# Norm sums taken per chunk, token-column roots, no barriers between dense stages, and modulation units in pairs

## The reference

```python
def rms_norm(x, g):
    y = x * lax.rsqrt(jnp.mean(x * x, axis=-1, keepdims=True) + RMS_EPS)
    return y * g

mod_l = jnp.split(c_act @ ada_w[l] + ada_b[l], N_MOD, axis=-1)   # and mod_c from cc_act
h_l = modulate(xl, norm_mix_g[l], mod_l[0], mod_l[1])            # norm(x) * g * (1 + scale) + shift
xl = xl + mod_l[2] * o_l
xl = xl + mod_l[5] * sq_relu_mlp(modulate(xl, norm_mlp_g[l], mod_l[3], mod_l[4]), w_mlp1[l], w_mlp2[l])
return rmsnorm(xl, final_norm_g)
```

## Time and profile before

| | us |
|---|---|
| median of 3 runs | 3123.83 (3122.11 to 3124.45) |
| the profiled execution | 3122.36 |
| its span in the trace | 3120.6 |
| PE busy | 2918.6 |
| DVE / ACT / POOL busy | 860.3 / 716.4 / 237.7 |

### The profile page before, as it was taken

The page is one execution under the profiler, slowest core; times in us unless marked ns, Lnnn a source line. Parts: engine busy times, 40 slices in busy tenths (PEclk is TensorE's granted clock), DMA queues, the critical chain, the costliest instruction groups (busy, mean ns, idle before and its releaser), DMA issues. The chain is left out here.

```text
span 3120.6 us, 30901 instructions
## 1 busy us (share of the span) xinstructions
PE 2918.6 (94%) x12390; PEld 1851.9 (59%) x12390; DVE 860.3 (28%) x1571; ACT 716.4 (23%) x1683; POOL 237.7 (8%) x260
## 2 busy tenths in 40 slices
PE   7989997999997999999989999997999799998998
PEld 6768884455554666444434444443666577787887
DVE  1421003545545333200121110004555523201101
ACT  1420002356455233100010000002454422201100
POOL 3000000223232000000000000000222200000000
PEclk8989998999998999899999999998999999999999
DMA  9328763433331221122214543333344222254552
GB/s 222 88 75 247 223 206 89 110 88 95 95 97 53 55 55 55 48 74 78 73 52 127 149 129 121 101 98 81 103 108 102 75 68 68 81 152 124 151 151 71
DMA packets 529871, 330.42 MB, mean 106 GB/s; under 512 B 27472, under 2 KB 496832, under 8 KB 529728
## 3 DMA queue, kind: packets, MB, share of 16 engines
q1 hardware_dynamic: 518896, 296.36, 33.5%
q0 software_dynamic: 10528, 31.46, 4.1%
q10 hardware_dynamic: 304, 0.61, 0.1%
HBM read 327.05 MB, written 1.34 MB: 105 GB/s over the span
## 5 line engine op out<-in xcount | busy, mean ns | idle before, releaser
L917 PE MATMUL ps<-xnT,W 128*128 128x512 f32 (+2 forms) x4064 | 1341.8, 490 | 65.6 <-ACTq L392 44.0
L917 PEld LDWEIGHTS ps<-xnT,W 128*128 128x128 f32 (+1 forms) x4064 | 776.9, 193 | 597.2 <-issue 469.7
L917 PE MATMUL ps<-BIG,W 128*128 128x256 f32 (+1 forms) x2528 | 773.5, 468 | 11.1 <-ACTq L392 8.5
L917 PEld LDWEIGHTS ps<-BIG,W 128*128 128x128 f32 x2528 | 481.2, 191 | 301.3 <-issue 247.3
L1733 DVE SCALAR_TENSOR_TENSOR TMP<-ps,prmT,TMP 128x510 f32<-128x510 f32 (+3 forms) x256 | 182.6, 714 | 140.9 <-ACT TMP L714 126.4
L552 ACT ACTIVATE xnT<-hT 128x256 f32<-128x256 f32 (+1 forms) x56 | 23.1, 495 | 630.8 <-DVEq L392 630.8
L1653 DVE SCALAR_TENSOR_TENSOR hT<-ps,modc,hT 128x256 f32<-128x256 f32 x48 | 21.7, 481 | 398.1 <-PE ps L917 398.1
L501 POOL DMA_DIRECT2D cs_rows<-BIG x2 | 1.1, 564 | 1693.9 <-DVE BIG L1775 1693.9
L1327 PE MATMUL ps<-W,xnT 128*128 128x128 f32 x1024 | 122.6, 276 | 0.0
L527 POOL TENSOR_TENSOR BIG<-BIG,TMP 128x512 f32<-128x512 f32 x80 | 108.2, 1367 | 186.7 <-ACT BIG L747 186.7
L546 ACT ACTIVATE TMP<-ps 128x512 f32<-128x512 f32 (+4 forms) x130 | 73.2, 569 | 208.7 <-PE ps L1327 94.3
(11 more groups left out here) (248 smaller groups left out, 2172.4 us busy)
## 6 DMA issues: line engine op xcount, KB each, us to landing
W<-in_w_in SPq DMA_DIRECT2D x192, 512.0 KB, 4.0
W<-in_w_mlp SPq DMA_DIRECT2D x128, 512.0 KB, 4.0
W<-in_ada_w SPq DMA_DIRECT2D x96, 512.0 KB, 4.9
BIG<-cs_rows POOLq DMA_DIRECT2D x96, 256.0 KB, 4.8
W<-in_w_ssd_o SPq DMA_DIRECT2D x32, 512.0 KB, 4.0
W<-in_w_gate SPq DMA_DIRECT2D x22, 512.0 KB, 8.3
W<-in_w_up SPq DMA_DIRECT2D x22, 512.0 KB, 6.5
W<-in_w_down SPq DMA_DIRECT2D x16, 512.0 KB, 4.1
```

The source lines that it names most:

```text
L917: last = mm(dst, w[:, c, 0:m], rhs(k), start=k == 0, stop=k == total - 1)
```

## The change

1. *Norms.* The square of a chunk is taken by ACT as soon as its residual is added (in `rooted`), and DVE adds the squares of chunks 0 to 6 into `ssum` between residuals (`summed`). After the last product, PE multiplies 128 token columns at a time, as the stationary side, by one column of ones (`statistic`): the sum over the width lands with one token per partition, in one column per 128 tokens. Root and reciprocal are taken of these 2 or 4 columns; DVE multiplies them into an identity (`diagonal`), and one product with ones spreads them over all partitions (`gap`). The scaling reads this from PSUM. ACT loads the table of the root ahead by a root of a constant.
2. *normf1 and mixnorm0 become one:* both statistics are taken from `hT` (with and without the gain), the second mean is made from the first in columns; the normed output of the first block is made in `hT` by POOL, in two multiplies of 128x2048.
3. *No barriers* but ahead of wout1, att0 and att1. The first product of a stage waits per chunk (`ready`).
4. *The end:* in f21 each chunk is multiplied by the gain and transposed one product later; the copies out of PSUM scale by the reciprocal, two on ACT and two on DVE, followed by four stores.
5. *Modulation units* go in pairs: seven pairs behind steps of dense stages (`MID`), five inside the norms (`GAP`). Inside a norm the rows of the first unit stand in PE's stream between statistic and spreading product, those of the second behind it; the columns follow after two products (or after the first of ssd). ACT copies the rows in place of DVE.

```diff
-ADA = {"ffn1": (0, 0, 8), "down1": (0, 8, 4), "f10": (1, 0, 8), "f20": (1, 8, 4)}
+BARRIERS = {"wout1": 3, "att0": 6, "att1": 9}
+MID = {("ffn1", 5): (0, 2), ("down1", 1): (0, 4), ("wout20", 0): (0, 8), ("f10", 2): (1, 0), ("f10", 5): (1, 2),
+       ("f20", 1): (1, 4), ("wout21", 0): (1, 8)}
+GAP = {"wout1": (0, 0), "down1": (0, 6), "wout20": (0, 10), "f20": (1, 6), "wout21": (1, 10)}
...
+            pool.wait_ge(r1_kept, 1)
+            pool.wait_ge(n_x, 16)
+            h0 = hT[:, :, 0:S]
+            nc.gpsimd.tensor_tensor(h0, h0, r1b[:, :].unsqueeze(1).to_broadcast([P, KC, S]), ALU.mult)
+            pool.drain()
+            nc.gpsimd.tensor_tensor(h0, h0, prmT[:, 0, 16:24].unsqueeze(2).to_broadcast([P, KC, S]), ALU.mult)\
+                .then_inc(h_ready, 1)
...
+            def rooted(ph, n, l=None, which=0):
+
+                A(small[:, 59:60], eps, ACT.Sqrt)
                 for c in range(KC):
+                    act.wait_ge(g_free, freed(ph, c))
+                    last = A(xnT[:, c, 0:n], hT[:, c, 0:n], ACT.Square)
+                    if ph == "down1":
+                        last = A(xnT[:, c, S:T], hT[:, c, 0:S], ACT.Square, scale=prmT[:, 0, 16 + c:17 + c])
+                    last.then_inc(n_sq, 1)
...
+                act.wait_ge(n_col, NORMS[ph] + 1)
...
+                    A(root[:, 0:m], stat[:, 0:m], ACT.Sqrt, scale=1.0 / D, bias=eps).then_inc(n_rt, 1)
+                if ph in GAP:
+                    row_copies(*GAP[ph], which=(0,))
+                if l is not None:
+                    for c in range(KC):
+                        act.wait_ge(n_x, 8 * NORMS[ph] + c + 1)
...
+                        last.then_inc(n_sh, 1)
+                if ph in GAP:
+                    row_copies(*GAP[ph], which=(1,))
...
+            def statistic(ph, m):
+
+                k = NORMS[ph]
+                stat = PS[6 if ph == "f21" else 3]
+                one = cst[:, C_ONE:C_ONE + 1]
+                pe.wait_ge(n_acc, k + 1)
+                for j in range(m):
+                    mm(stat[:, j:j + 1], ssum[:, j * P:(j + 1) * P], one, start=j == 0, stop=False)
+                pe.wait_ge(n_sq, 8 * k + 8)
+                for j in range(m):
+                    last = mm(stat[:, j:j + 1], xnT[:, KC - 1, j * P:(j + 1) * P], one, start=False, stop=j == m - 1)
+                last.then_inc(n_col, 1)
+
+            def gap(ph, m, n):
+
+                l, u = GAP[ph]
+                statistic(ph, m)
+                ada_rows(l, u)
+                pe.wait_ge(n_dg, NORMS[ph] + 1)
+                mm(PS[3][:, 0:n], ones, diag[:, 0:n // P, :].rearrange("p a b -> p (a b)"), start=True, stop=True)\
+                    .then_inc(n_bc, 1)
+                if ph == "down1":
+                    mm(PS[6][:, 0:S], ones, flat(diag1), start=True, stop=True).then_inc(r1_ps, 1)
+                ada_rows(l, u + 1)
...
-                product([("dt", l)], PS[4][0:64, :], xa, 64)
+                product([("dt", l)], PS[4][0:64, :], xa, 64, ready=shifted("f20" if l else "down1"))
...
+            def summed(ph, c, n):
+
+                if c == 0:
+                    return
+                dve.wait_ge(n_sq, 8 * NORMS[ph] + c + 1)
+                if c > 1:
+                    dve.drain()
+                last = V.tensor_tensor(ssum[:, 0:n], xnT[:, 0, 0:n] if c == 1 else ssum[:, 0:n], xnT[:, c, 0:n], ALU.add)
+                if c == KC - 2:
+                    last.then_inc(n_acc, 1)
```

More of the change, by code:

```diff
@@ L322, in build @@
         g1_t, g1_e = sem("gain1_transposed"), sem("gain1_kept")
-        x_sq, x_ms, x_rt, x_sc, x_t, x_e = (
-            [sem(f"x_{n}{t}") for t in range(2)] for n in ("squares", "mean", "root", "scaled", "transposed", "kept"))
+        x_sq, x_ms, x_rt, x_sc, x_t = (sem(f"x_{n}") for n in ("squares", "mean", "root", "scaled", "transposed"))
+        x_e = [sem(f"x_kept{t}") for t in range(2)]
         p_done, p_kept, p_added = sem("piece_done"), sem("piece_kept"), sem("piece_added")
@@ L328, in build @@
         line_ps, line_sb, line_out, bias_in = sem("line_ps"), sem("line_sb"), sem("line_out"), sem("bias_in")
-        n_sq, n_sum, n_ms, n_rt, n_x = (sem(f"norm_{x}") for x in ("squares", "sum", "mean", "root", "scaled"))
+        n_sq, n_acc, n_col, n_rt, n_ms, n_dg, n_bc, n_x, n_sh = (
+            sem(f"norm_{x}") for x in ("squares", "summed", "columns", "root", "second_mean", "diagonal", "spread",
+                                       "scaled", "shifted"))
+        r1_ps, r1_kept, h_ready = sem("first_root_spread"), sem("first_root_kept"), sem("first_normed")
+        n_hg, out_a, out_v = sem("end_gained"), sem("out_by_scalar"), sem("out_by_vector")
         u_sc, u_mx, u_ex, u_pn, u_tp, u_pt, u_pv, u_out = (
@@ L672, in _ @@
             begin(act, "wout1")
-            end(act)
-            squares("norm2", S)
-            end(act)
-            begin(act, "ffn1")
+            rooted("wout1", T)
             for i in range(FC1 // 2):
@@ L1246, in _ @@
                 front(0, 0)
+                pair(ada_columns, GAP["f20" if l else "down1"])
                 front(0, 1)
@@ L1440, in _, with from_merge @@
-            norm("normend", S)
-            begin(pe, "out")
-            for t in range(2):
-                for half in range(2):
-                    for c in range(4):
-                        last = nc.tensor.transpose(PS[2 * t + half][:, c * P:(c + 1) * P],
-                                                   xnT[:, 4 * half + c, t * P:(t + 1) * P], ident)
-                    last.then_inc(out_t, 1)
-            end(pe)
+                def from_merge(k):
+                    pe.wait_ge(m_free, 8 * l + k + 1)
@@ new lines, in _, with transposed @@
+                gap(f"wout2{l}", nt // P, nt)
+                dense(f"f1{l}", 8, single(f"f1{l}"), lambda t: PS[4 + t][:, 0:nt], xn, ready=shifted(f"wout2{l}"),
+                      gapped=f"wout2{l}")
+                def transposed(c):
+                    pe.wait_ge(n_hg, c + 1)
+                    for t in range(2):
+                        last = nc.tensor.transpose(PS[2 * t + c // 4][:, (c % 4) * P:(c % 4 + 1) * P],
+                                                   xnT[:, c, S + t * P:S + (t + 1) * P], ident)
+                    last.then_inc(out_t, 1)
@@ L1770, in masked @@
                             .then_inc(ssd[l, "mready"], 1)
+                adds(*GAP["f20" if l else "down1"])
                 conv(0, 0)
```

389 lines of the change are left out of this document (210 added, 179 removed).

## The result

The changed kernel takes 3001.94 us (median of four runs, 2997.00 to 3004.68) against 3124.14 us for the kernel before (3122.11 to 3125.69): a ratio of 0.9606, 95% interval 0.9591 to 0.9621, or 122.2 us less. The prediction was 3011.0 us, range 2999 to 3034. The profiled execution has a span of 3001.1 us, 119.5 us less than the span of the one before.

The account below looks back on a forecast made before the run. TensorE, busy 2918.6 of 3120.6 us, was taken as the bound. 153.15 + 11.7 - 34.8 - 6.5 - 1.7 - 5 - 4 = 112.85 us less gives 3011.0 us; 8-in-10 range 2999 to 3034.

Parts of the forecast that it names:

- the forecast's own case: Whole kernel: all terms act as summed, 112.85 us less, 3011.0 us, range 3003 to 3020; chance 0.58.
- rival C: Whole kernel: no port conflict or clock loss, less half clock behind dt chain (some 5 us); 2997 us; chance 0.10.
- The norms' chain: Five gaps between dense stages: first products start 6.4, 8.0, 7.3, 7.3 and 5.8 us in, sum 34.8 us.
- rival B: Gaps of the norms: new chain slower than summed, 3 us a gap, total 3026 us; chance 0.17.
- Rival E: Change fails to do what it says, e.g. first products stay behind eighth chunk: 5.7 us more a gap, 3040; chance 0.05.
- The clock in the gaps: Five new gaps: light work drops TensorE's clock in two, 2 us each, 4 in all; bounds 0 and 10.
- Rival A: Five gaps: each wholly at half clock, with loss behind it, 34 us in place of 4, 3041 us; chance 0.08.
- The end: Tail after the last product: 18.42 us become 6.5; transposes moved into f21 cost TensorE 1.7 us.
- The modulation units and short barriers: TensorE outside the gaps: moved units free 11.7 us; five short stretches, mostly bare barriers, 10.55 us, go to zero.
- rival D: Tile ring: refills one behind another at 4.9 us starve unit pairs, 315 us over twelve, 3326 us; chance 0.01.
- GpSimd's multiplies: Start of ssd0: two 2048-column multiplies delay VectorE's dt chain, which TensorE awaits, by 5 us; bounds 0 and 10.2.
- The test named in the prediction's last part: Profile after: if the gaps are as summed and the total is not, a stretch outside the tabled windows has grown.

Follow-up runs that it names:

- the split rows: Against the changed kernel, two of the first unit's four row tiles in each norm issued ahead of the last chunk's statistic: 3001.89 us, ratio 0.9604.
- the repeated kernel: The changed kernel itself, unedited, run and profiled again on another chip: 3000.77 us median, ratio 0.9608, profiled span 2994.8 us.

## Why the prediction was right, and where it was off

The forecast of 112.85 us less stands against 119.5 in the profiled pair and 122.2 in the medians. The measured 3001.94 us lies in the range of 2999 to 3034, but 1 us outside the 3003 to 3020 of the forecast's own case, and nearer to rival C's 2997 than to 3011.0. Set out by place, its terms compare so (the 0.3 us that miss from 112.85 are rounding):

| place | forecast, us less | measured, us less |
|---|---|---|
| the six stretches (130.33) | 85.0 (34.8 + 4 + 6.5 left) | 80.4 (42.6 + 7.3 left) |
| dense stages | 35.4 | 37.6 |
| stages with SSD and attention | -7.9 | 1.5 |
| sum | 112.5 | 119.5 |

The misses have opposite signs: the stretches gave 4.6 us less than forecast, the long stages 9.4 more. That the total came out within 9 us is in part luck.

*The norms' chain.* Right in its parts. Of the 7.8 us by which the five gaps exceed 34.8, some 6.1 are the clock and 1.7 the chain. Without half clock the first, third and last gap read 6.67, 7.76 and 6.06 us for 6.4, 7.3 and 5.8, so the forecast is 0.3 to 0.5 us too low each; rival B had 3. The miss in the third is ahead of the unit rows: the last chunk's statistic starts 1.8 us behind the last product, not 1.5. That chunks arrive fast enough for the products is right: none waits behind a gap, and undoing the per-chunk start costs 26 us. Undoing the early squares costs 43. The second gap (8.0 forecast) had half clock in both profiles, 9.40 and 9.35; at full clock it reads 8.22 in the kernel with the barriers restored. Rival E is excluded by the gaps themselves, and its price was nearly right: 28.5 us, five times 5.7, against 26 in the kernel that does what it describes, where the waits were 5.3 to 5.7 us in three norms and about 2 in the two others.

*The clock in the gaps.* The mechanism was right, the size a little low. Forecast were two of five gaps at 2 us, 4 in all. The first profile has three gaps at about 1.64 and one at 1.2, some 6.1 us; the second has two, 2.8. Rival A (all five cold throughout) did not come: only the first unit's rows and what is beside them fall to the lower level, and the split rows remove even that. The loss behind the gaps, 12.27 us, went in full, as summed. So the sign that the prediction named, windows of 0.50 behind the gaps, did not come, and the loss lies inside them.

*The end.* 7.3 us for 6.5. The copies are done 3.6 us behind the first one-column product, with which the stretch begins (3.4 summed); the span ends 3.7 us later (3.1 summed). The four stores are issued one behind the other, and it is 3.1 us from the last issue, not from the last copy, to the end. VectorE's and the queue's rows of the end:

```profile
2995.95 1.41 DVE L2044 TENSOR_SCALAR TMP<-ps,small 128x512 f32<-128x512 f32 x2
2996.60 0.36 SPq L455 DMA_DIRECT2D out<-TMP  x1
...
2997.98 0.45 SPq L457 DMA_DIRECT2D out<-TMP  x1
```

*The modulation units and short barriers.* Right. By the prediction's terms the dense stages lose 12 units' rows at 1.92 and 4 units' columns at 0.95 (26.8 us; 22 and 20 units stood there, 10 and 16 do now), 7.6 us of clock and 2.7 of barriers, and gain 1.7 of transposes: 35.4, measured 37.6. The barriers restored wait for 7.0 us, as the short stretches had been without the unit in one of them; the kernel loses 9.8. A unit pair costs TensorE 3.64 + 1.84 us where it stands in a dense stage, as the rows of before said. Ring starvation (rival D) is not seen anywhere: no product waits for a load in the table of waits.

*GpSimd's multiplies.* Forecast 5 us, measured 4.83 in the two VectorE steps and 4.8 in TensorE's wait. The size is in part luck. The first multiply was 1.9 us old (of 4.50) when the chain's second step came, much as expected, and cost it 2.4 us. The second was expected right behind the first, to meet a gap of the chain. By the trace 4.09 us without a releaser lie between the two (the same in all profiles of the changed kernel, 1.2 us where the multiplies come late; the cause is open), so the second stood beside line 1813, which has two SBUF inputs, and cost another 2.4. Right behind the first it would have ended at 484.4 and been over before line 1813 began at 485.98, an estimate from these rows. The 4.6 us that the prediction worked out by the rule of the Trainium skill's page "SBUF — State Buffer" were nearer than its 1.5 by the rows alone, but counted a wait of the one-input step, and here that step ran between the multiplies and waited for neither.

*What was missing.* The long stages should have become 7.9 us longer (11.5 for four units' rows and four uncovered columns, 5 for the port, less 4.7 of clock and 3.9 of barriers); they became 1.5 shorter. 9.4 us are thus outside the steps as summed. TensorE's time at half clock in these three stages is 122.0 us before and 95.6 after. Some 9 of the 26.4 us were in the forecast (24.54 behind the gaps, less 15.2 that lie in the dense stages), so 17 us at half clock are left, worth up to 8.5. Windows over the work behind TensorE's wait for the dt chain, layer 0 and layer 1, before and then after, show where 10.2 of them went:

```profile
549.90:560.20 10.30, 7.29 (x16) 3.47 (x17) 6.63 (x10) 0.77 (x2) 0.00 (x0) 0.50 0.10 30
2157.50:2164.40 6.90, 4.88 (x6) 2.18 (x7) 4.71 (x7) 0.04 (x1) 0.00 (x0) 0.51 0.00 0
```
```profile
497.50:504.50 7.00, 4.28 (x12) 2.44 (x13) 6.36 (x10) 0.77 (x2) 0.00 (x0) 0.51 0.00 0
2052.60:2063.00 10.40, 7.90 (x32) 3.65 (x32) 5.57 (x8) 1.24 (x4) 0.00 (x0) 1.00 0.19 50
```

Behind the chains 17.1 us at half clock became 6.8, in both profiles of the changed kernel, which is up to 5.1 us. This is the step that rival C named, with its price of some 5 us for both layers; C's other two steps, no port conflict and no clock loss, did not come. In layer 1 the columns (1.84 us) and the earlier table load take up the wait of 3.3 us and no half clock follows; in layer 0 the wait of 4.9 us beside GpSimd's multiplies is left, with 6.8 us at half clock behind it, and in the kernel with the multiplies late alone there is neither. The table load, which the prediction did not look at, is worth 1.3 us in layer 1. That leaves about 3 us, for which there are 6.8 us less at half clock elsewhere in the stages; why is not settled. Part of that is the chance that the repeated kernel shows.

The test named in the prediction's last part held: the gaps are about as summed and the total was lower, so a stretch outside of the earlier trace rows had shrunk. About half of what it gave beyond the forecast was the clock behind the waits for the dt chain.

## What to carry to other kernels

Ahead of a norm's statistic, have all squares but the last taken and added beside the products (43 us here), start the next products chunk by chunk (26 us), and put dense products that are needed anyway into the gap, ahead of the step that waits for a small engine. Then look at what stands on the shared path of VectorE and GpSimd at that moment: a long GpSimd operation without a deadline belongs where VectorE has no chain that TensorE waits for. When an edit of 5 us is judged, compare the windows of the stages it touches; the total moves by as much through the clock alone.

## What the runs showed of the hardware

- Two executions of the same kernel differed by 6.3 us in span with 10.0 us less at half clock; a gap of 7.76 us in one was 9.40 in the other. In the third gap the lower clock was on the work behind the one-column products.
- Unit rows on either side of the last one-column products kept the granted clock at 1.00 in five of five gaps in both kernels that have them (35.66 and 35.64 us), where rows behind them alone kept it in one of five and three of five in two profiles of the same kernel.
- A VectorE operation with two SBUF inputs that starts inside a GpSimd multiply of 2048 columns ended 0.5 to 0.6 us behind that multiply, at each start seen: 3.08 us in one kernel and 1.74 in another that reaches it 1.4 us later.
- ScalarE's table load (1.28 us) ran while the data of its activation was still awaited, and where it stood hung on the order in which two waits were written; TensorE's wait for the chain was 0.05 us in one order and 1.38 in the other.
- GpSimd's two multiplies of 128x2048 (4.50 and 3.60 us) stood 4.09 us apart with nothing awaited that the profile shows, and 1.2 us apart where they came late.
